# A first weight tile loaded behind the second row chunk, a first projection in three passes, and two output-projection groups opened over seven of eight parts

## The reference: what is computed

```python
h = rmsnorm(x, norm_mix)
z, xbc_raw, dt_raw, q, k, v, gl_ssm, gl_sb = split_cols(h @ w_in)
...                                   # SSD branch -> y_ssm, stick-breaking attention -> y_sb
merged = sigmoid(gl_ssm) * y_ssm + sigmoid(gl_sb) * y_sb
x = x + merged @ w_out
...                                   # memory cross-attention, then a 16-expert MoE
```

## Time and profile before

| | us |
|---|---|
| three runs, median (lowest to highest) | 1203.53 (1202.56 to 1205.54) |
| the profiled execution's own time | 1205.74 |
| its span, first to last instruction | 1204.0 |
| PE busy | 1144.2 (95%) |
| DVE busy | 715.8 (59%) |
| ACT busy | 564.6 (47%) |
| share of PE in the chain that ended last | 73% |

### The profile page before, as it was taken

One profiled execution on the slowest core, in us unless ns is written; L12 is line 12 of the kernel. 1 busy time (PEld: TensorE's weight loads), 2 busy tenths in 40 slices (PEclk: granted clock), 3 DMA queues, 4 the chain that ended last, 5 costly groups with the idle time before them and its releaser, 6 DMA issues.

```text
span 1204.0 us, 18490 instructions
## 1 busy us (share of the span) xinstructions
PE 1144.2 (95%) x7908; PEld 1035.7 (86%) x7908; DVE 715.8 (59%) x850; ACT 564.6 (47%) x709; POOL 120.6 (10%) x147
## 2 busy tenths in 40 slices
PE   4999999999999999999899999999899999999994
PEld 4998779999987899999899999989757878788873
DVE  4424574775368743332434743534679998888884
ACT  4424473334386731221313632311166868778763
POOL 2002341000134100000000000000001000000051
PEclk9999998999999999999999999999899999999998
DMA  9231110222310222332435612201799999999995
GB/s 292 85 131 36 36 40 1 89 88 72 79 45 2 71 71 79 97 85 74 149 100 195 214 53 71 71 1 36 274 356 379 421 416 381 387 402 390 368 267 151
DMA packets 95038, 197.27 MB, mean 164 GB/s; under 512 B 4208, under 2 KB 71960, under 8 KB 82664
## 3 DMA queue, kind: packets, MB, share of 16 engines
q1 hardware_dynamic: 87328, 169.88, 40.2%
q0 software_dynamic: 5440, 18.76, 5.4%
q10 hardware_dynamic: 2184, 7.39, 1.5%
HBM read 178.41 MB, written 17.61 MB: 163 GB/s over the span
## 4 chain that ended last, share of the span: by engine, by line
PE 73%; DVE 10%; ACT 8%; issue 4%; DMA 4%; ACTq 0%; SPq 0%; POOL 0%; DVEq 0%; POOLq 0%
PE ps L2241 46%; PE ps L1032 6%; DVE buf_r L966 4%; ACT buf_r L959 3%; PE ps L1042 3%; PE ps L2646 2%; PE ps L2662 1%; DMA buf<-in_w_gate_e 1%; PE ps L2344 1%; PE ps L2373 1%; DMA buf<-in_w_in 1%; DVE buf_r L1181 1%; ACT buf_r L461 1%; PE ps L2374 1%; PE ps L2386 1%
## 5 line engine op out<-in xcount | busy, mean ns | idle before, releaser
L2241 PE MATMUL ps<-buf_r,buf_r 128*128 128x288 f32 (+1 forms) x4560 | 603.0, 293 | 12.8 <-DVE buf_r L465 6.5
L2241 PEld LDWEIGHTS ps<-buf_r,buf_r 128*128 128x128 f32 x4560 | 590.9, 190 | 17.3 <-issue 9.2
L966 DVE TENSOR_TENSOR buf_r<-buf,buf_r 128x2048 fp32r<-128x2048 f32 x92 | 205.1, 2284 | 0.0
L1032 PE MATMUL ps<-buf_r,buf_r 128*128 128x512 f32 x720 | 174.6, 398 | 0.0
L959 ACT CAST buf_r<-buf 128x2048 fp32r<-128x2048 f32 x92 | 170.9, 1908 | 0.1
L446 DVE TENSOR_TENSOR buf_r<-buf,buf_r 128x2048 fp32r<-128x2048 f32 (+2 forms) x49 | 107.5, 2196 | 103.8 <-ACT buf_r L440 103.7
L1032 PEld LDWEIGHTS ps<-buf_r,buf_r 128*128 128x128 f32 x720 | 133.4, 188 | 29.5 <-issue 0.5
L440 ACT CAST buf_r<-buf 128x2048 fp32r<-128x2048 f32 (+2 forms) x53 | 96.6, 1824 | 109.1 <-PE ps L2241 55.1
L1042 PE MATMUL ps<-buf_r,buf_r 128*128 128x512 f32 x384 | 89.8, 390 | 0.5 <-DVE buf_r L1209 0.5
L1042 PEld LDWEIGHTS ps<-buf_r,buf_r 128*128 128x128 f32 x384 | 72.0, 188 | 15.8 <-DVE buf_r L1209 0.9
L461 ACT CAST buf_r<-ps 128x512 fp32r<-128x512 f32 (+2 forms) x41 | 30.0, 731 | 75.9 <-PE ps L1016 63.2
(11 more groups left out here) (331 smaller groups left out, 1269.8 us busy)
## 6 DMA issues: line engine op xcount, KB each, us to landing
buf<-in_w_gate_e SPq DMA_DIRECT2D x32, 1024.0 KB, 8.3
buf<-in_w_up_e SPq DMA_DIRECT2D x32, 1024.0 KB, 7.9
buf<-in_w_down_e SPq DMA_DIRECT2D x32, 1024.0 KB, 7.4
buf<-in_w_in SPq DMA_DIRECT2D x16, 1024.0 KB, 5.5
buf<-in_w_in SPq DMA_DIRECT2D x17, 512.0 KB, 4.9
buf<-in_w_mem_kv SPq DMA_DIRECT2D x8, 1024.0 KB, 5.9
y_rows<-buf ACTq DMA_DIRECT2D x14, 512.0 KB, 8.0
buf<-in_x_prompt SPq DMA_DIRECT2D x8, 512.0 KB, 5.6
```

The lines of the kernel that those rows point to most:

```text
L966: nc.vector.tensor_tensor(e_lo(t), e_raw(t), e_hi(t), ALU.subtract).then_inc(wl_ready, 1)
L1032: last = nc.tensor.matmul(bank(b), r32(a[:, k, :]), w[:, i, :], start=(k == 0 and j == 0), stop=(k == KD - 1 and j == 2))
L2241: last = nc.tensor.matmul(out, a, b, start=(k == 0 and j == 0), stop=(k == len(parts) - 1 and j == 2))
```

## The change

At the start SP issues the loads of chunks 0 and 1, then tile 0, then chunks 2, 3 and 4, then tile 1. On ACT `split_high(0)` moves from behind the factor of chunk 2 to behind that of chunk 1, and `split_high(1)` from behind `act_ht(4)` to ahead of `act_ht(3)`. On DVE tile 0's low part and chunk 0's `tokens_low` move ahead of `gain(1)`, and the later steps follow chunk by chunk. On PE the first group `kv(0)` moves ahead of `turn(2)`, and each later `turn` stands one group later relative to the groups; `kv(0)` goes through its eight parts three times, once for each kind of product, with a wait ahead of each pass.

At the output projection PE opens groups 0 and 1 and goes through seven of their eight parts as soon as seven parts of `MG` are split, and finishes both with the eighth part when that is there. The other 18 groups stay as they were.

```diff
-            load_rows(XS)
+            load_first(0)
+            load_first(1)
             load(0)
+            load_first(2)
+            load_first(3)
+            sp.dma_start(XS[:LS, 4, :], I["x_sample"][0]).then_inc(x_loaded[4], 16)
             load(1)
...
-                if i == 2:
+                if i == 1:
                     split_high(act, 0)
                 if 2 <= i < 5:
                     act_ht(i - 2)
                 if i == 4:
+                    split_high(act, 1)
                     act_ht(3)
                     act_ht(4)
-                    split_high(act, 1)
...
             gain(0)
+            split_low(dve, 0)
+            tokens_low(0)
             gain(1)
             scale(2)
-            split_low(dve, 0)
-            tokens_low(0)
+            tokens_low(1)
             gain(2)
             scale(3)
-            tokens_low(1)
-            gain(3)
-            scale(4)
             dve.wait_ge(vec_psum, 2)
             nc.vector.tensor_copy(CTXT, bank(6)[:, 128:164]).then_inc(vec_ready, 1)
             tokens_low(2)
+            gain(3)
+            scale(4)
+            tokens_low(3)
             gain(4)
-            tokens_low(3)
             tokens_low(4)
...
             turn(1)
+            def kv_first():
+                out = bank(4)[:, 0:256]
+                high, low = ([r32(f[:, k * T:k * T + P]) for k in range(KD)] for f in (HTH_F, HT_F))
+                pe.wait_ge(wh_ready, 1)
+                pe.wait_ge(ah_ready, A_HT + 1)
+                for k in range(KD):
+                    nc.tensor.matmul(out, high[k], w_hi(0)[:, k, :], start=(k == 0), stop=False)
+                pe.wait_ge(wl_ready, 1)
+                for k in range(KD):
+                    nc.tensor.matmul(out, high[k], w_lo(0)[:, k, :], start=False, stop=False)
+                pe.wait_ge(al_ready, A_HT + 1)
+                for k in range(KD):
+                    last = nc.tensor.matmul(out, low[k], w_hi(0)[:, k, :], start=False, stop=(k == KD - 1))
+                last.then_inc(kv_psum, 1)
+
+            kv_first()
             turn(2)
...
-            for i in range(10):
-                t, m = divmod(i, 5)
-                if i in (1, 2):
-                    turn(i + 2)
+            for i in range(1, 10):
+                t, m = divmod(i, 5)
+                if i in (2, 3):
+                    turn(i + 1)
...
+            def out_part(m, k0, k1):
+                for k in range(k0, k1):
+                    mh, ml = w_hi(W_O)[:, k, :], w_lo(W_O)[:, k, :]
+                    for j, (a, b) in enumerate(((MGH_F, mh), (MGH_F, ml), (MG_F, mh))):
+                        last = nc.tensor.matmul(bank(m)[:, 0:256], st_m(a, k, m), b, start=(k == 0 and j == 0),
+                                                stop=(k == KD - 1 and j == 2))
+                return last
+
+            pe.wait_ge(gs_ready, KD)
+            pe.wait_ge(wl_ready, W_O + 1)
+            pe.wait_ge(al_ready, A_MG + KD - 1)
+            out_part(0, 0, KD - 1)
+            out_part(1, 0, KD - 1)
             pe.wait_ge(al_ready, A_MG + KD)
-            for i in range(4 * NC_):
+            out_part(0, KD - 1, KD).then_inc(wo_psum, 1)
+            out_part(1, KD - 1, KD).then_inc(wo_psum, 1)
+            for i in range(2, 4 * NC_):
```

More of the change, by code:

```diff
@@ L1452, in load, with load_first @@
                     sp.dma_start(tile_view(RAW[n % NRAW], n)[:, k0:k0 + src.shape[1], :], src).then_inc(ring_loaded[n % NRAW], 16)
-            load_rows(XS)
+            def load_first(m):
+                sp.dma_start(XS[:, m, :], xr[:, m, :]).then_inc(x_loaded[m], 16)
+            load_first(0)
+            load_first(1)
             load(0)
+            load_first(2)
+            load_first(3)
+            sp.dma_start(XS[:LS, 4, :], I["x_sample"][0]).then_inc(x_loaded[4], 16)
             load(1)
@@ L2284, in _, with kv @@
             turn(1)
+            def kv(i, b):
+                t, m = divmod(i, 5)
+                rproj(b, W_K + t if t < 2 else W_V + t - 2, m, HTH_F, HT_F).then_inc(kv_psum, 1)
+            def kv_first():
[13 more added lines that the diff above has]
+            kv_first()
             turn(2)
@@ L2287, in _ @@
             nc.tensor.transpose(bank(6)[:, 128:164], CTXR[0:36, :], IDENT[0:36, 0:36]).then_inc(vec_psum, 1)
-            def kv(i, b):
+            for i in range(1, 10):
                 t, m = divmod(i, 5)
-                rproj(b, W_K + t if t < 2 else W_V + t - 2, m, HTH_F, HT_F).then_inc(kv_psum, 1)
-            for i in range(10):
-                t, m = divmod(i, 5)
-                if i in (1, 2):
-                    turn(i + 2)
+                if i in (2, 3):
+                    turn(i + 1)
                 if i == 2:
@@ L2579, in _ @@
                     tproj(4, nb, 0, ZSH, ZS).then_inc(br_psum, 1)
+            st_m = lambda flat, k, m: r32(flat[:, k * T + m * P:k * T + m * P + P])
+            def out_part(m, k0, k1):
[10 more added lines that the diff above has]
+            out_part(1, 0, KD - 1)
             pe.wait_ge(al_ready, A_MG + KD)
-            for i in range(4 * NC_):
+            out_part(0, KD - 1, KD).then_inc(wo_psum, 1)
+            out_part(1, KD - 1, KD).then_inc(wo_psum, 1)
+            for i in range(2, 4 * NC_):
                 t, m = divmod(i, NC_)
```

## The result

The changed kernel takes 1192.45 us in the median of five runs (1190.92 to 1195.38), the kernel before 1203.53 beside it: a ratio of 0.9907 (95% interval 0.9890 to 0.9923). A second comparison of the same two kernels gave 1195.89 against 1203.95 (0.9924, 0.9907 to 0.9941): 8.1 us less, inside that range.

What follows compares the result with a forecast made beforehand. PE, busy 95% of the span, was taken to bound the kernel. The start's -1.95 us and the output projection's -4.8 summed to -6.75, giving 1196.8 us against the median of 1203.53, with a range of 1194.0 to 1199.8.

Steps and rivals of the forecast that it cites:

- What bounds the kernel, and where the gain comes from: Whole kernel: PE, busy 95% of the span, bounds it; gains come from its idle or 1.2 GHz time at two places.
- The output projection: Output projection: 42 matmuls move into PE's wait; -4.8 us, 3.2 from the wait and 1.6 from the pace.
- the stretch at 0.50 comes anyway: Rival, output projection: PE doesn't idle but a stretch at 0.50 follows; -3.2 instead of -4.8, 1198.4 us, chance 0.08.
- The start: Start: group 4 starts 2.85 us earlier, less 0.9 for a possible fall of the clock; -1.95 us.
- The landings: Start, first loads: tile 0 lands at 10.8 us by bytes, chunk 2 at 13.5 by interpolation.
- lands sooner, at the rows' rate: Rival, start: tile 0 lands at 9.3, chunk 2 at 10.7; another 1.0 us, 1195.8 us, chance 0.09.
- The pace of the first group: Start, PE: the first group takes 5.1 us as before, most of it at half pace.
- The fall of the clock behind the wait: Start: PE idles some 2.1 us ahead of group 4; a fall would cost 1.7, taken as 0.9.
- The row of 1.70 without a fall: Profile row behind the start's clock term: behind 1.70 us idle PE kept its pace, 33 matmuls in 4.3 us.
- the row of 2.26 with one: Profile row behind the start's clock term: behind 2.26 us idle the clock was 0.50 for 3.41 us.
- The slower rival: Rival, start: tile 0 ahead of chunks 2 to 4 on three lists delays group 4; 1207.2 us, chance 0.03.
- the one that the order buys little: Rival, start: tile 0 falls into the slow stretch, chunk 2 lands at 17; 1198.2 to 1199.5 us, chance 0.15.

Runs made afterwards that it cites:

- e3: Kernel before, with GpSimd's two loads of the router weights issued behind tile 1's landing: 1204.25 us against 1204.82 (0.9992).
- e9: Kernel before, with the edit of e3 and SP's load of the 64 rows issued behind tile 1 too: 1199.59 us, taken once.
- e1: Kernel before, with only the start's part of the change and its output groups as they were: 1199.35 us against 1204.82 (0.9959).
- e6: Changed kernel, with the first group in one pass of 24 that waits for both low parts: 1195.39 us, ratio 0.9930.
- e4: Changed kernel, with GpSimd's two loads of the router weights issued behind tile 1's landing: 1195.45 us, ratio 0.9911.
- e5b: Changed kernel, with SP's old order of loads: 1199.89 us against 1204.11 (0.9966).
- e7: Changed kernel, with ACT's factors of the two memory chunks moved behind its copies of groups 0 and 1: 1193.92 us, ratio 0.9917.
- e11: Changed kernel run again without an edit, for a second comparison and a second trace: 1195.89 us (0.9924).

## Why the prediction was wrong, point by point

**What bounds the kernel, and where the gain comes from: right.** Both places, and the terms' nature, stood up; the parts alone take about 5 us each and add.

**The output projection: right.** -4.8 forecast, -5.0 in the trace: the wait of 3.2 us and the half pace behind it both went, with the eighth part ready before PE asked for it and DVE's first addition ahead of the fifth output group. The rival that the stretch at 0.50 comes anyway fell in all nine traces with this part.

**The start: the mechanism right, the size wrong, -1.95 for -5.3** (-4.1 in the second trace of the changed kernel). Three terms were off.

The landings, 1.75 us. I let tile 0 land when the same number of bytes had landed before (10.8; it came at 9.7) and chunk 2 by interpolation (13.5; 11.9), "since they hold the slow stretch as it stood". That was the step that failed: the slow stretch isn't a property of the byte count. e3 and e9 show its makers, the router weights on GpSimd's own queue and the 64 rows, and tile 0 now goes ahead of the latter. Of the two landings chunk 2's is the one that counts: ACT, with tile 0's high part done at 11.62, waits for it 0.27 us and rounds chunk 0 behind its factor. The first group started at 14.68 instead of 16.4, and at 14.89 in the second trace. The rival "lands sooner, at the rows' rate" (9.3, chance 0.09) was the true case for tile 0; its bound of 10.7 for chunk 2 wasn't reached, as that chunk met the stretch. In the prediction that rival was also held back by the gains' transposition, which I took to stay at 12.22. It came at 9.3 or 9.4 in every trace with the new order, at 11.1 to 12.2 with the old one and at 9.66 in e9, which has no slow stretch that early. So that gate moved with the same stretch.

The pace of the first group, 0.75 us from its start to the fifth. I gave it the 5.1 us of before. In this execution the clock was 0.50 for 3.41 us only (15.02 to 18.43), and from its start to the next transposition the group took 4.4 us. By the same measure it took 4.9 before, 4.4 in e1, 5.0 in e6 and 5.3 in e4 and in the second trace of the changed kernel. So this part of the 5.3 is luck of the execution, not a gain of the three passes.

The fall of the clock behind the wait, 0.9 us. The wait was 1.73 us instead of 2.1, and 1.00 stayed. That wait is 1.72 or 1.73 in the traces of the changed kernel (twice), e1, e4, e5b and e6, and no time at 0.50 follows it in any. The row of 1.70 without a fall held as well, in all fourteen traces; the row of 2.26 with one didn't, with a fall in nine of them. Had the wait been the 2.1 us of the forecast, these runs wouldn't tell on which side it would have come out.

**The sum and the range.** With -5.3 and -5.0 the sum is -10.3; measured were -11.1 and, the second time, -8.1. The second lies inside the range, so on which side of its low end one comparison falls is in part luck. The start's size was wrong all the same, as e1 shows with 5.5 us for the start alone. The spread of the stretches at 0.50 from 60 us on, 1 to 5 at 1.4 us each in single executions, is wider than the "some 1 us" that the range allowed for, and the range's low end was one rival off its middle, when the misses of the start added up. Two numbers of the prediction don't follow from its own terms, and neither enters the sum or the range: the start's end of -4.1 (-2.85 and the first rival's 1.0 give -3.85), and the 10.6 by the fit for tile 0 of before, counted from the first load's issue at 0.81. From the tile's own issue at 3.33, as the 8.5 is counted from 1.7, it is 13.1; 16.28 is later than either.

**The slower rival, and the one that the order buys little: wrong.** Every trace with the new order has tile 0 by 11.1. e5b shows the price that the slower rival named: with tile 0 late, ahead of chunks 2 to 4 on three lists, the fifth group comes 2.2 us later than before.

## What to carry to other kernels

A load's landing isn't to be read off a count of bytes: ask which transfers made the slow slices, and whether they will still be ahead. An earlier transfer is worth what the first engine in line makes of it, so the loads' order and the engines' lists have to move together. One trace isn't enough to price a microsecond: count what differs between two executions of the same kernel first. Work that is ready can be opened over all of its parts but the last to cover a wait, and where a stretch at half pace follows that wait, it goes too.

## What the runs showed of the hardware

- While a load of 256 KB into 64 partitions is under way, all loads together run at 165 to 194 GB/s for some two microseconds (e3), and these slow slices move when that load moves (e9).
- Two loads of 80 KB in all, in pieces of 16 and 64 bytes on another queue, came with a landing of tile 0 1.7 us later than without them (before, e3).
- Tile 0 landed between 9.2 and 11.1 us with one and the same order of SP's loads (e1, e4, e6, e7, e11).
- The number of stretches at 0.50 between 60 us and the last merge product was 3 and 4 in two executions of one kernel, and the time between two fixed points goes by 1.4 us for each (fourteen traces).
- Time at 0.50 followed one and the same wait of PE of 2.26 us in nine of fourteen traces. It followed waits of 1.69 to 1.73 us in none, and the wait of 3.2 us at the output projection in all five that have it.
